# Attention scores on TensorE: mask first in one matmul a map, score matmuls alternating between the halves of the partitions

## The reference

```python
q = rotary(rms_norm(q, q_norm_w, NORM_EPS), pos)      # (1, 256, 32, 64): map m of head h is 2h + m
k = rotary(rms_norm(k, k_norm_w, NORM_EPS), pos)
for i in range(s // Q_BLOCK):                          # two blocks of 128 queries
    q0 = i * Q_BLOCK
    kv = q0 + Q_BLOCK                                  # 128 keys for the first, 256 for the second
    sc = einsum('bqhd,bkhd->bhqk', q[:, q0:kv], k[:, :kv]) * scale
    mask = arange(kv)[None, :] <= (q0 + arange(Q_BLOCK))[:, None]
    sc = where(mask, sc, -inf)
    pr = softmax(sc, axis=-1).reshape(b, H, 2, Q_BLOCK, kv)
    wts = pr[:, :, 0] - lam * pr[:, :, 1]
    outs.append(einsum('bhqk,bkhe->bqhe', wts, v[:, :kv]))
```

## Time and profile before

| | |
|---|---|
| time, median of 3 runs | 2181.34 us (2179.87, 2181.34, 2187.02) |
| profiled execution, first to last instruction | 2180.0 us; no other time is given for it |
| busy, share of the span | PE 99%, PEld 92%, DVE 58%, ACT 47%, POOL 6% |
| mean granted clock of TensorE | 0.998 of 2.4 GHz |
| read from HBM | 387.24 MB, 179 GB/s over the span |
| head stage | from about 283 to 544 us |

### The profile page before, as it was taken

The page is one execution under the profiler, slowest core; times in us unless marked ns, Lnnn a source line. Parts: engine busy times, 40 slices in busy tenths (PEclk is TensorE's granted clock), DMA queues, the critical chain, the costliest instruction groups (busy, mean ns, idle before and its releaser), DMA issues.

```text
span 2180.0 us, 38469 instructions
## 1 busy us (share of the span) xinstructions
PE 2163.7 (99%) x14801; PEld 2003.1 (92%) x14801; DVE 1265.7 (58%) x1408; ACT 1017.2 (47%) x1280; POOL 135.6 (6%) x165
## 2 busy tenths in 40 slices
PE   9999999999999999999999999999999999999999
PEld 8888889989999888888999999899999999998887
DVE  6676445555766777777654555555555555554443
ACT  5444444555446555555553333453433434443332
POOL 1111000000001222222000000000000000000000
PEclk9999999999999999999999999999999999999999
DMA  6656755544566555555565555566566665656664
GB/s 220 206 179 208 203 166 149 150 136 141 161 191 193 177 179 173 177 179 177 171 213 189 179 183 189 187 176 183 177 188 182 183 183 173 192 184 202 195 203 142
DMA packets 206331, 394.63 MB, mean 181 GB/s; under 512 B 15602, under 2 KB 20387, under 8 KB 205747
## 3 DMA queue, kind: packets, MB, share of 16 engines
q1 hardware_dynamic: 203778, 385.00, 58.0%
q0 software_dynamic: 2336, 8.46, 1.2%
q10 hardware_dynamic: 144, 0.20, 0.0%
HBM read 387.24 MB, written 2.16 MB: 179 GB/s over the span
## 4 chain that ended last, share of the span: by engine, by line
PE 93%; DVE 3%; issue 3%; ACT 1%; DMA 0%; DVEq 0%; SPq 0%; ACTq 0%
PE acc L1271 55%; PE acc L1257 31%; PE side L1359 2%; DVE w_lo L723 2%; PE side L1287 2%; PE side L1481 1%; DVE conv_x L833 1%; PE side L1362 0%; DVE yT L1002 0%; ACT w_hi L412 0%; PE side L1487 0%; DMA rows<-in_subln_w 0%; PE side L1435 0%; PE side L1377 0%; PE side L1379 0%
## 5 line engine op out<-in xcount | busy, mean ns | idle before, releaser
L723 DVE TENSOR_TENSOR w_lo<-w_raw,w_hi 128x1024 fp32r<-128x1024 f32 x712 | 901.3, 1273 | 778.4 <-ACT w_hi L412 774.5
L412 ACT ACTIVATE w_hi<-w_raw 128x1024 fp32r<-128x1024 f32 x712 | 751.1, 1058 | 1006.4 <-PE acc L1271 629.6
L1271 PE MATMUL acc<-x2T_hi,w_hi 128*128 128x256 f32 x1408 | 398.6, 283 | 0.0
L1271 PE MATMUL acc<-x2T_hi,w_lo 128*128 128x256 f32 x1408 | 398.5, 283 | 0.0
L1271 PE MATMUL acc<-x2T_lo,w_hi 128*128 128x256 f32 x1408 | 398.5, 283 | 0.0
L1271 PE MATMUL acc<-h_hi,w_hi 128*128 128x256 f32 x1280 | 371.9, 291 | 0.0
L1271 PE MATMUL acc<-h_lo,w_hi 128*128 128x256 f32 x1280 | 362.6, 283 | 0.0
L1271 PE MATMUL acc<-h_hi,w_lo 128*128 128x256 f32 x1280 | 362.5, 283 | 0.0
L1271 PEld LDWEIGHTS acc<-x2T_lo,w_hi 128*128 128x128 f32 x1408 | 270.3, 192 | 0.0
L1271 PEld LDWEIGHTS acc<-x2T_hi,w_hi 128*128 128x128 f32 x1408 | 270.3, 192 | 0.0
L1271 PEld LDWEIGHTS acc<-x2T_hi,w_lo 128*128 128x128 f32 x1408 | 270.3, 192 | 0.0
(11 more groups left out here) (226 smaller groups left out, 2776.5 us busy)
## 6 DMA issues: line engine op xcount, KB each, us to landing
w_raw<-in_w_in SPq DMA_DIRECT2D x320, 512.0 KB, 4.0
w_raw<-in_w_ffn_gate SPq DMA_DIRECT2D x88, 512.0 KB, 3.7
w_raw<-in_w_ffn_up SPq DMA_DIRECT2D x88, 512.0 KB, 4.0
w_raw<-in_w_ffn_down SPq DMA_DIRECT2D x88, 512.0 KB, 4.2
w_raw<-in_w_ssm_proj SPq DMA_DIRECT2D x64, 512.0 KB, 4.0
w_raw<-in_w_attn_proj SPq DMA_DIRECT2D x32, 512.0 KB, 4.3
w_raw<-in_w_out SPq DMA_DIRECT2D x32, 512.0 KB, 4.2
acs_b<-acs_scratch POOLq DMA_DIRECT2D x16, 512.0 KB, 5.9
```

The source lines that it names most:

```text
L412: nc.scalar.activation(w_hi[:, r], w_raw[:, r], ACT.Copy).then_inc(hi_ready, 1)
L723: nc.vector.tensor_tensor(w_lo[:, r], w_raw[:, r], w_hi[:, r].bitcast(F32), ALU.subtract).then_inc(lo_ready, 1)
L1271: done = nc.tensor.matmul(out_at, w[:, r, kk, cut], a[:, k0 + kk], start=first and kk == n == 0 and c % 2 == 0, stop=last and kk == UK - 1 ...
```

## The change

`mask_b` becomes a tile of three blocks of 128 columns, [mask, zeros, mask], at another address. For each map one matmul of 384 columns writes it into the bank first (start=True), before any score. The four score matmuls then add to it, ordered by query block first and map second, so that they alternate between partitions 0 to 63 and 64 to 127. Nothing else differs.

```diff
-        mask_b = at("mask_b", 82.25, [P, P], BF16)
+        mask_b = at("mask_b", 207, [P, 3, P], BF16)
...
-                nc.vector.tensor_copy(mask_b[:], mask_in[:]).then_inc(setup_done, 1)
+                nc.vector.memset(mask_b[:, 1], 0.0)
+                nc.vector.tensor_copy(mask_b[:, 0], mask_in[:])
+                nc.vector.tensor_copy(mask_b[:, 2], mask_in[:]).then_inc(setup_done, 1)
...
                 for m in range(2):
-                    half = slice(m * DH, (m + 1) * DH)
-                    for q in range(TT):
-                        first, width = q * P, (q + 1) * P
-                        nc.tensor.matmul(side[:, 1 + m, first:first + width], qkT[half, 0, q * P:(q + 1) * P],
-                                         qkT[half, 1, 0:width], start=True, stop=False)
-
-                        last = nc.tensor.matmul(side[:, 1 + m, first + width - P:first + width], ident_b[:], mask_b[:],
-                                                start=False, stop=True)
+                    nc.tensor.matmul(side[:, 1 + m, 0:3 * P], ident_b[:], mask_b[:].rearrange("p n k -> p (n k)"), start=True, stop=False)
+                for q in range(TT):
+                    first, width = q * P, (q + 1) * P
+                    for m in range(2):
+                        half = slice(m * DH, (m + 1) * DH)
+                        last = nc.tensor.matmul(side[:, 1 + m, first:first + width], qkT[half, 0, q * P:(q + 1) * P],
+                                                qkT[half, 1, 0:width], start=False, stop=q == TT - 1)
                 last.then_inc(scores, 1)
```

## The result

| | before | changed |
|---|---|---|
| time, median | 2180.75 us (4 runs, 2179.87 to 2187.02) | 2158.92 us (4 runs, 2158.20 to 2159.52) |
| profiled execution, span | 2180.0 us | 2156.8 us |
| ratio | | 0.9897, 95% interval 0.9885 to 0.9909 |

The change is 21.8 us faster, 1.0%.

The account below looks back on a forecast made before the run. TensorE, busy 99% of the span, was taken as the bound; fewer drains, bare loads and mask costs plus partly overlapped streams saved 0.96 us a head, times 16 heads 15.4, giving 2166.0 us, range 2160.5 to 2172.5.

Parts of the forecast that it names:

- TensorE bounds, all of it comes off the end: Head stage: TensorE waits only 1.7 us, so whatever it no longer does shortens the span if other engines keep up.
- 0.09 us of drain and a bare load of 0.11 for each change of rows: Head's score block: switching between 64-row and 128-row matmuls empties the array for 0.09 us, then an unhidden 0.11 load.
- Masks, 0.32 a head: Head's mask: two added matmuls of 384 columns, estimated at 0.16 us each, replace four of 128 columns.
- from first stream to last that is 1.07: Head's four scores: streams overlap but loads come one at a time, 1.07 us instead of 1.28.
- the rival with overlapping loads: Head's four scores: loads of the two halves overlap too, streams 0.87 us, 18.6 us gained, 2162.7; chance 0.23.
- loads never stand closer than 0.11 here: Score loads in the trace: objection to overlapping loads, claiming a least spacing of 0.11 us.
- rival 3: Head's four scores: loads overlap as well as streams, 18.6 us gained, 2162.7 us; chance 0.23.
- Range: Whole kernel: 2160.5 (overlapping loads, the clock's 1.5 us, a little spread) to 2172.5 (no overlap plus run spread).
- everything in both halves at once, loads too: Head's four scores: the full-overlap bound on side-by-side matmuls, against 1.28 us of streams in a row; written out as 0.87.
- Rival 4: Head's scores: each change of half costs 0.09 + 0.11, giving back 9.6 us, 2178.9, no tellable change; chance 0.12.
- Rival 5: Head stage: clock falls after heads, up to 24 us lost against 12 gained, 2193; chance 0.03.
- Setup: Kernel start, VectorE: an added memset and cast, about 0.3 us, hidden by VectorE's lead and costed at 0.

Follow-up runs that it names:

- e2: Changed kernel with all four scores of a head reading partitions 0 to 63, map 0 replacing map 1; 2168.29 us.
- e1: Changed kernel, masks still first, but scores in the old order, both of map 0 and then both of map 1; 2158.43 us.
- e8: The kernel before, unchanged, profiled once more; 2179.65 us (one run), span 2178.0.
- e3: Changed kernel with scores alternating, but the mask behind them as four 128-column matmuls, in two pairs; 2161.17 us.
- e4: Changed kernel with the mask matmuls left out, so no causal mask is applied; 2153.62 us.
- e5: Changed kernel with its two 384-column mask matmuls moved behind the scores; 2156.47 us.
- e6: Changed kernel with masks behind the scores, each one matmul of 256 columns without the block of zeros; 2155.47 us.

## Why the prediction was right and wrong

- **TensorE bounds, all of it comes off the end**: right. The wait for prob stayed at 1.7 us, no wait for w_lo or for weights appeared in the head stage, and the shift stays constant to the end.
- **0.09 us of drain and a bare load of 0.11 for each change of rows**: right. In the changed kernel the last streams start at 287.82, end 0.21 later, and the transposes' bare load starts at 288.13, 0.09 after that. With the halves' overlap taken away by e2, the gain was 11.5 us where the drains, loads and masks alone had been put at 12.0.
- **Masks, 0.32 a head**: 0.34 measured by leaving them out.
- **"from first stream to last that is 1.07"**: this step failed. It was written out in program order, map 0's second pass ahead of anything of map 1, and even the rival with overlapping loads (0.87) kept that order. The run has 0.64: loads in both halves at once, and map 1's first pass beside map 0's first. e2 shows that the halves do it (10.3 us for 0.64 a head), e1 that program order does not bind them. The term was 0.43 too large a head, 16 x 0.43 = 6.9 us, and 15.4 + 6.9 = 22.3.
- **"loads never stand closer than 0.11 here"**, the reason for 1.07 and against rival 3: true of the loads of the scores, but not of the whole trace of before. Behind the last mask of the first head two loads start 0.016 us apart:

```profile
289.42 0.10 PEld L1362 LDWEIGHTS side<-mask_b,ident_b 128*128 128x128 bf16 x1 [0.33 <-issue]
289.43 0.31 PEld L1287 LDWEIGHTS side<-cst,qk_row 128*128 128x128 f32 x3
```

  Both are loads of 128 rows, so they do not price the halves; they do show that 0.11 was no least distance.
- The small rest: three heads (11, 12 and 15) begin behind a wait (that of head 12 is only 0.14 us), in which their first drain had been hidden before. Against e8 they gain 1.29 instead of 1.39, 0.3 us in all, and 22.3 becomes 22.0, beside 21.8 measured.
- **Range**: its low end was the 0.87 case plus the clock. That case kept the same program order as the 1.07, so it was no bound. The prediction named the full bound in words ("everything in both halves at once, loads too") but put 0.87 on it. Half of the streams gone is 1.28 / 2 = 0.64 and would have given 2159; it could be had from the rows, as nothing in them spoke of an order between halves.
- **Rival 4**, a drain at each change of half: excluded, the pairs start 0.006 us apart. The Trainium skill, page TensorEngine Tiling (Array Packing), section Key Properties, ties the drain to a change of the mode and not of the tile, and with e1 and the change the trace now agrees on both halves of that.
- **Rival 5**, the clock: excluded. The changed kernel's granted clock is 1.00 in the head stage. Also my reading that the fall after head 11 came of the kernel's wait there was not borne out by the second profile of the same kernel. And "else 2.4" was wrong of the first one: it has a second stretch at 0.50, from 12.2 to 15.6 us, in the start of the program.
- **Setup**: the memset took 0.11 us. What follows on VectorE starts at 36.05 instead of 35.82, of which 0.09 is that the first cast starts later (35.64 instead of 35.55), so the memset and the cast cost 0.14 and not 0.3; the projection matmuls behind did not shift. Right in what it cost the kernel.

The Trainium skill, page TensorE: Matmul & The Clock Gate, section Part 3: Packing small matmuls, has matmuls of distinct row groups start about 4 ns apart; here it is 6 in the change, which is near, and 13 in e1. The same section says that matmuls start and end strictly in program order. e1 contradicts that for matmuls in different halves, and by that rule its time would have been 6.9 us longer; the measurement decides.

## What to carry to other kernels

Matmuls that use only 64 rows should stand together in the program, with nothing of 128 rows between them: each alternation costs a drain and a bare load (0.2 us here), and it keeps the two halves of the array from working side by side. Here fewer alternations and fewer, longer masks were worth 11.5 us together, the halves side by side 10.3. In which order the four scores stand inside such a group did not matter. When a sum is bounded by an overlap that no row shows, take the full overlap as the bound, not the overlap that an assumed order allows.

## What the runs showed of the hardware

- Two halves of the rows run two-pass fp32 matmuls in lockstep, loads included: eight records in four pairs, 0.64 us of streams where one half alone needs 1.28 (the change and e2: 10.3 us in 16 heads).
- Map 1's first pass started 0.013 us after map 0's first although three more matmul records of map 0 stood ahead of it in the program (e1).
- A matmul of 128 rows between them stops this: in the kernel before, no two score matmuls of different maps are ever paired, and a mask matmul stands between each; in e3, scores on either side of the masks don't pair either.
- One pass of 256 fp32 score columns takes 0.21 us (starts at 287.870 and 288.086 in e2), a projection matmul of 256 columns 0.12 (286.721 to 286.843 in the change), and a score makes two such passes.
- One profile of the kernel before had 3.4 us at half clock in the head stage, another had none, at a price of 1.4 us. Five of the eleven profiles (before, e1, e4, e5 and e6) also have 3.4 us at half clock between 10.9 and 15.6 us, and in these the first projection matmul starts at 17.4 to 18.3 us, in the others at 16.8 to 17.5. What sets such a fall off is open; no run was made to find out.
